# A two-block transformer kernel: own buffers for the first conditioning slabs, and a new order of the work around the first pair of heads

## The chip, the cores and the metric

The kernel runs on one core of a Trainium2 chip. The metric is the device time of one execution in microseconds, as the median of several runs. Beside it there is one profiled execution, whose trace gives the start, the length and the releaser of each instruction.

## The reference

The first block has two layers, the second block one. All tokens: T = 512, width 1024. Layer 0, where the change lies, is a gated delta rule with conditioning:

```python
c_act = jax.nn.silu(c)
mod = c_act @ ada_w[layer] + ada_b[layer]          # 6 parts of 1024
shift_m, scale_m, gate_m, shift_f, scale_f, gate_f = split(mod, 6)
h = rmsnorm(x, norm_mix_g) * (1.0 + scale_m) + shift_m
# gdn_mixer(h): q, k, v, gate, beta and decay are projections of h
#   q, k, v pass a causal convolution of 4 taps and silu; q and k are l2-normed
#   chunked gated delta rule over 8 heads of 128:
#   S_t = exp(g_t)(I - beta_t k_t k_t^T) S_{t-1} + beta_t k_t v_t^T ;  o_t = S_t^T q_t
#   o = rmsnorm(o, norm_g) * silu(gate) ; return o @ w_out
x = x + gate_m * y
h = rmsnorm(x, norm_ffn_g) * (1.0 + scale_f) + shift_f
x = x + gate_f * swiglu(h, w_gate, w_up, w_down)
```

Behind it come a layer of latent attention with its own FFN, and the second block (retention, sliding-window attention, FFN).

## The kernel before, in words

**Slabs.** All weights are cut into slabs of 128 x 2048 fp32 (1 MB). SyncE loads slab s into raw[s % 2] (load_slab, L418), once the low part of slab s - 2 is made. ScalarE copies it to fp32r as its high part (split_hi, L300), once the products of slab s - 2 are done; VectorE subtracts to make the low part (split_lo, L306); TensorE does three matmuls for each 128 x 128 block (lo*H, hi*L, hi*H). A slab is 16 steps of three matmuls in layer 0: eight for its first half (bank half m = 0) and eight for its second (m = 1).

**Conditioning.** There are 48 slabs of ada_w. The first eight (shift_m and scale_m) gate the first norm. TensorE multiplies them by silu(c) held in a padded tile, cpad (first_rows_pe L338, copied by first_act L364, turned into columns by first_cols_pe L356), in four groups g of two slabs. Groups 0 and 2 use the two buffers adar, groups 1 and 3 the tile go, so groups 2 and 3 are loaded only once groups 0 and 1 are through (load_first L371). The other 40 are done on GpSimd: a product by silu(c) and three halving sums per slab (ada_chunks L311, L315 and L317); TensorE then adds over the partitions by four small matmuls (ada_pe L408). Their two buffers are again adar, loaded by load_ada (L424) once TensorE is through with the slab two before. Six such slabs belong to each pair of heads, 24 in all, and 16 to the first FFN. GpSimd begins when gg["tsc"] is signalled (L2056).

**The start.** ScalarE squares the eight chunks of x, TensorE sums them (norm_pe L433), ScalarE takes logarithm and exponential (norm_act L453); norm_first_dve (L384) applies norm, scale and shift group by group and writes hL, ScalarE hH. Squares, norm and padded tile lie in tiles that the pairs use later (fs, kbT, pb, dt).

**The first product and the gates.** Slab 0 yields the raw gates of all eight heads. rows_dve_1 to _4 (L629 to L675) and three activations turn them into cumulative decay and beta, by eight-partition instructions; rows_dve_3 (L648) is ten of them in a chain. rows_pe (L682) transposes them, tsc_dve (L677) stores them, and SyncE spreads them over the partitions through DRAM (rows_out L690, row_in L698) into dt, dtb and qd.

**Pairs of heads.** gdn_pe (L1110), gdn_act (L705) and gdn_dve (L896) hold an order written out by hand. The projections of q, k, v and gate are 16 slabs of 16 steps, 256 steps; the generator product_steps (L1091) yields after each step, and fill(n) (L1114) puts n steps between the other instructions of TensorE. A step at a slab's beginning waits for its low part, and each half for its bank: that is the convolution (conv L900 on VectorE: four taps, from PSUM) of the same half of the slab before it. Slabs 1, 2, 3 are q, k, v of pair 0; 4, 5, 6 those of pair 1; 7 is the query of pair 2. Before pair 0 there are 64 steps (slabs 1 to 4), then 48 in each of pairs 0, 1, 2 and 48 in pair 3.

A pair p (loop at L1138) starts, when the key is scaled (gg["kn"]), with the gram products of the keys (L1153). Six levels then invert a triangular matrix: TensorE multiplies (L1185), ScalarE copies (pb_copy, zz_copy L784 to L790), TensorE multiplies (L1213), VectorE copies under a mask (level L970). Fillers stand on both sides of L1213 (lv_fill). After these come four rounds t over the chunks: value, state product (L1250), output (L1257, L1258), with the state updated by VectorE (state L1000). Meanwhile convolution, activation, sum of squares (sum_squares L1118: square on ScalarE, matmul with ones, Ln into fln, Exp into fex) and scaling (q_norm L929, k_norm L936) prepare pair p + 1. At the end the output norm's two sums (L1274) share one bank, W: the second waits for the logarithm of the first (gg["oln"]).

Of the kernel before, what the change touches and what calls it, by code (L numbers as in the profile page):

```python
# [46 lines left out]
ADA_SKEW = 4  # L47
# [71 lines left out]
def build(nc, slabs, ada, vecs, consts, masks, rope, vbias, pos, xin, out):  # L119
# [4 lines left out]
    with ctx:  # L124
# [29 lines left out]

        gdn = ExitStack()
        lvl = sb("lvl", [P, 7 * P], i32, gdn)
# [19 lines left out]
        go = sb("go", [P, KC, T], scope=gdn)  # L176
        rows, rtmp = go[0:GH, 0:4, :], go[0:GH, 4:7, :]
        cpad = dt[:].rearrange("p m t -> p (m t)")[:, 0:KC * 32].rearrange("p (k n) -> p k n", k=KC)
# [58 lines left out]
        go_in, go_done = [sem("go_in0"), sem("go_in1")], sem("go_done")  # L237
# [96 lines left out]
        def row_summed(eng, g, h):  # L334

            eng.wait_ge(go_done if g % 2 else ada_done, g // 2 * 2 + h + 1)

        def first_rows_pe(pe, g, h):  # L338

            a = Slab(g // 2 * 2 + h)  # L340
            if g % 2:
                pe.wait_ge(go_in[h], a.prior(1, 16))
                w3 = go[:, 4 * h:4 * h + 4, :].rearrange("p c t -> p (c t)")
            else:
                pe.wait_ge(ada_in[h], a.prior(1, 16))
                w3 = adar[h]
# [7 lines left out]
            last.then_inc(go_done if g % 2 else ada_done, 1)  # L354

        def first_cols_pe(pe, g, h):  # L356

            pe.wait_ge(row_ready, 2 * g + h + 1)
            for m in range(2):
                last = T_.matmul(first_bank[g][:, 2 * h + m:2 * h + m + 1], st[:, 2 * h + m, :], ones[:, 0:1],  # L360
                                 start=True, stop=True)
            last.then_inc(first_col, 1)

        def first_act(act, g):  # L364

            for h in range(2):
                row_summed(act, g, h)
                S_.activation(st[:, 2 * h:2 * h + 2, :].rearrange("p a n -> p (a n)"), row_bank[h],
                              ACT.Copy).then_inc(row_ready, 1)

        def load_first(sp, g):  # L371

            for h in range(2):
                src = ada[ADA_FIRST[g][h], :, :]
                if g % 2:
# [329 lines left out]
        def gdn_act(act):  # L705
# [59 lines left out]
            for m in range(2):  # L765
                silu(vs, 3, m)
            split_hi(act, Slab(5))

            for p in range(GH // 2):
# [38 lines left out]

                for m in range(2):
# [66 lines left out]
                w("op", p + 1)  # L876
                for m in range(2):
                    S_.activation(up[:, m, :], D[2][:, m, :], ACT.Square, scale=P ** -0.5).then_inc(gg["osq"], 1)
                    S_.activation(go[:, 2 * p + m, :], D[2][:, m, :], ACT.Copy,
                                  scale=vec[:, V["gdn_g"]:V["gdn_g"] + 1]).then_inc(gg["osq"], 1)  # L880
# [4 lines left out]
                nle()  # L885
                for m in range(2):
                    w("oss", 2 * p + m + 1)
                    S_.activation(vT[:, m, :], D[0][:, 1, :] if not front and m else W, ACT.Ln,
                                  bias=eps).then_inc(gg["oln"], 1)
                for m in range(2):  # L890
                    w("oln", 2 * p + m + 1)
                    S_.activation(vT[:, m, :], vT[:, m, :], ACT.Exp, scale=-0.5).then_inc(gg["oex"], 1)
# [3 lines left out]
        def gdn_dve(dve, chain):  # L896
# [213 lines left out]
        def gdn_pe(pe):  # L1110
# [23 lines left out]
            w("fln", 3)  # L1134
            sum_squares(xi, 1, 4)
            fill(12)

            for p in range(GH // 2):  # L1138
# [4 lines left out]
                lv_fill = 2 if front else 3  # L1143
# [34 lines left out]
                for lv in range(1, 7):  # L1178
# [36 lines left out]
                    if lv in (1, 3, 5):  # L1215
                        ada_at(lv // 2)
# [11 lines left out]
                for t in range(NT):  # L1228
# [1075 lines left out]
```

## Time and profile before

| | |
|---|---|
| median of 3 runs | 2621.35 us (2618.05 to 2631.58) |
| the profiled execution | 2633.81 us, its span 2632.0 us |
| TensorE, matmul | 2433.5 us busy (92%), 11504 instructions |
| VectorE | 1126.2 us (43%) |
| ScalarE | 900.9 us (34%) |
| GpSimd | 354.7 us (13%) |
| DMA | 259.7 MB, mean 99 GB/s |
| chain that ended last | TensorE 73%, issue 10%, GpSimd 7%, VectorE 6%, ScalarE 3% |

Busy time is the sum over an engine's instructions; it doesn't say which of them the end waits for. An "x" with a number is a count of instructions; a releaser in brackets is what ended the idle time before the row. The profile takes a span on the device, and the time of the execution lies 1.8 us above it.

### The profile page before, as it was taken

The page shows a single profiled execution, that of the slowest core. Times are in us where ns is not written, and L with a number is a line of the kernel's source. Part 1 is how long each engine was busy: PE and PEld are TensorE (multiplying, and loading weights), DVE is VectorE, ACT ScalarE, POOL GpSimd, SP SyncE. Part 2 cuts the span into 40 slices and gives each one's busy share as a digit, 9 for nine tenths or more (in the row PEclk, how much of TensorE's full clock was granted, in tenths as well). Part 3 has the DMA queues.
Part 4 walks back from the last instruction along what each step waited for, and adds up shares of the span by engine and source line. Part 5 has one row for each costly group of instructions (what it writes and reads, how often), then busy time and mean ns, then how long its engine had stood idle before and what let it go on. Part 6 is the DMA issues. An engine that isn't in the chain of part 4 may idle for free.

```text
span 2632.0 us, 28942 instructions
## 1 busy us (share of the span) xinstructions
PE 2433.5 (92%) x11504; PEld 1929.2 (73%) x11504; DVE 1126.2 (43%) x1186; ACT 900.9 (34%) x1086; POOL 354.7 (13%) x164
## 2 busy tenths in 40 slices
PE   7899999989999978889999998999987798999997
PEld 4688888768888855567888886877865586788886
DVE  3956754543322464444333235343246524433234
ACT  4455453333311244333332124333234422432122
POOL 0345574357700000000000000000000000000000
PEclk8899999989999988889999998999998799999999
DMA  6324332335422313221222222122210022222222
GB/s 237 135 104 149 124 121 81 108 133 190 161 96 96 112 48 114 94 80 64 96 96 96 96 96 104 62 67 76 96 48 19 32 94 80 80 96 93 99 80 96
DMA packets 38430, 259.72 MB, mean 99 GB/s; under 512 B 4280, under 2 KB 4536, under 8 KB 8144
## 3 DMA queue, kind: packets, MB, share of 16 engines
q1 hardware_dynamic: 38352, 258.59, 27.6%
q8 instruction: 60, 0.98, 0.2%
q14 instruction: 18, 0.15, 0.0%
HBM read 256.42 MB, written 2.15 MB: 98 GB/s over the span
## 4 chain that ended last, share of the span: by engine, by line
PE 73%; issue 10%; POOL 7%; DVE 6%; ACT 3%; DMA 1%; POOLq 0%; DVEq 0%; ACTq 0%; SPq 0%
PE D L260 18%; PE D L261 18%; PE D L262 18%; POOL adar L317 4%; POOL adar L315 3%; PE D L275 3%; PE D L276 3%; PE D L277 3%; PE D L1453 1%; PE D L296 1%; PE D L297 1%; PE D L295 1%; PE D L1452 1%; PE D L1469 1%; DVE lo L308 1%
## 5 line engine op out<-in xcount | busy, mean ns | idle before, releaser
L308 DVE TENSOR_TENSOR lo<-raw,hi 128x2048 fp32r<-128x2048 f32 (+1 forms) x185 | 420.8, 2274 | 463.6 <-ACT hi L304 463.4
L260 PE MATMUL D<-hH,lo 128*128 128x512 f32 x1456 | 585.7, 402 | 0.0
L261 PE MATMUL D<-hL,hi 128*128 128x512 f32 x1456 | 575.4, 395 | 0.0
L262 PE MATMUL D<-hH,hi 128*128 128x512 f32 x1456 | 575.2, 395 | 0.0
L304 ACT ACTIVATE hi<-raw 128x2048 fp32r<-128x2048 f32 (+1 forms) x185 | 342.9, 1853 | 494.3 <-PE D L262 282.9
L260 PEld LDWEIGHTS D<-hH,lo 128*128 128x128 f32 x1456 | 275.1, 189 | 70.4 <-issue 8.0
L261 PEld LDWEIGHTS D<-hL,hi 128*128 128x128 f32 x1456 | 275.2, 189 | 66.6 <-issue 4.0
L262 PEld LDWEIGHTS D<-hH,hi 128*128 128x128 f32 x1456 | 274.7, 189 | 65.0
L317 POOL TENSOR_TENSOR adar<-adar 128x1024 f32<-128x1024 f32 (+2 forms) x120 | 201.8, 1681 | 9.4
L315 POOL TENSOR_TENSOR adar<-adar,cact 128x2048 f32<-128x2048 f32 x40 | 153.0, 3825 | 357.1 <-DMA adar<-in_ada 263.1
L261 PE MATMUL D<-aL,hi 128*128 128x512 f32 x444 | 176.0, 396 | 0.0
L260 PE MATMUL D<-aH,lo 128*128 128x512 f32 x444 | 176.0, 396 | 0.0
L262 PE MATMUL D<-aH,hi 128*128 128x512 f32 x444 | 176.0, 396 | 0.0
L1311 ACT ACTIVATE aH<-af 128x1024 f32 x33 | 35.0, 1060 | 326.3 <-DVE af L1328 326.3
L1328 DVE TENSOR_TENSOR af<-sg,D 128x1024 f32<-128x1024 f32 x33 | 40.3, 1222 | 203.9 <-PE D L262 203.9
L275 PE MATMUL D<-hH,lo 128*128 128x512 f32 x192 | 84.0, 437 | 47.1 <-DVE hL L482 32.6
L1103 PE MATMUL D<-hH,lo 128*128 128x512 f32 x256 | 117.2, 458 | 2.1 <-ACT qs L782 2.1
L506 DVE SCALAR_TENSOR_TENSOR x<-D,mod,x 128x512 f32<-128x512 f32 (+1 forms) x48 | 34.6, 748 | 176.2 <-PE D L262 149.7
L1105 PE MATMUL D<-hH,hi 128*128 128x512 f32 x256 | 102.8, 402 | 0.0
L1104 PE MATMUL D<-hL,hi 128*128 128x512 f32 x256 | 102.7, 401 | 0.0
L1307 ACT ACTIVATE sg<-D 128x1024 f32<-128x1024 f32 x33 | 33.9, 1027 | 200.0 <-PE D L262 160.9
L262 PEld LDWEIGHTS D<-aH,hi 128*128 128x128 f32 x444 | 83.6, 188 | 20.4
(374 smaller groups left out, 3518.2 us busy)
## 6 DMA issues: line engine op xcount, KB each, us to landing
raw<-in_slabs SPq DMA_DIRECT2D x185, 1024.0 KB, 4.8
adar<-in_ada SPq DMA_DIRECT2D x44, 1024.0 KB, 4.8
go<-in_ada SPq DMA_DIRECT2D x4, 1024.0 KB, 11.6
x<-in_xin SPq DMA_DIRECT2D x1, 2048.0 KB, 14.2
dt<-bcast SPq DMA_DIRECT2D x8, 256.0 KB, 3.4
dtb<-bcast SPq DMA_DIRECT2D x8, 256.0 KB, 4.3
qd<-bcast SPq DMA_DIRECT2D x8, 256.0 KB, 7.5
out<-x SPq DMA_DIRECT2D x1, 2048.0 KB, 6.3
```

The costliest lines, as they stand in the source:

```text
L260: T_.matmul(o, lo[s.slot][:, w], H[:, k, :], start=(k == 0), stop=False)
L261: T_.matmul(o, hi[s.slot][:, w], L[:, k, :], start=False, stop=False)
L262: last = T_.matmul(o, hi[s.slot][:, w], H[:, k, :], start=False, stop=(k == kc - 1))
L275: T_.matmul(o, lo[s.slot][:, w], H[:, k, :], start=(k == 0), stop=False)
L276: T_.matmul(o, hi[s.slot][:, w], L[:, k, :], start=False, stop=False)
L304: S_.activation(hi[s.slot][:, 0:n], raw[s.slot][:, 0:n], ACT.Copy).then_inc(hi_ready, 1)
L308: V_.tensor_tensor(lo[s.slot][:, 0:n], raw[s.slot][:, 0:n], hi[s.slot][:, 0:n], ALU.subtract).then_inc(lo_ready, 1)
L315: chain.link(nc.gpsimd.tensor_tensor(r3, r3, cact[:].unsqueeze(2).to_broadcast([P, KC, 2 * P]), ALU.mult))
L317: last = nc.gpsimd.tensor_tensor(r3[:, 0:n], r3[:, 0:n], r3[:, n:2 * n], ALU.add)
L1103: T_.matmul(o, lo[s % 2][:, c], hH[:, k, :], start=(k == 0), stop=False)
L1104: T_.matmul(o, hi[s % 2][:, c], hL[:, k, :], start=False, stop=False)
L1105: last = T_.matmul(o, hi[s % 2][:, c], hH[:, k, :], start=False, stop=(k == KC - 1))
```

## The change

1. The eight first slabs: two in adar, six in a new tile fw, each with its own semaphore, so that none waits for a buffer. Squares, norm rows, norm output, padded tile and copied rows have tiles of their own (xsq, xnt, xrs, cpad, arow), which all lie where the pairs' tiles lie later. SyncE loads x ahead of the slabs; TensorE sums the squares ahead of group 0. adar is used by two slabs fewer before GpSimd's, so ADA_SKEW and ADA0 change.
2. ScalarE makes the high part of slab 2 ahead of the exponential of the gates, VectorE the low part of slab 3 ahead of rows_dve_3.
3. TensorE does 44 + 4 steps ahead of pair 0 and 64 in it (three fillers in place of two, later places for the sums, the conditioning after levels 2, 4 and 6 instead of 1, 3 and 5). The second half of pair 0's value, and the whole query of pair 1, are convolved inside pair 0, and the high and low part of slab 5 are made there.
4. GpSimd waits for gg["kn"] in place of gg["tsc"].

```diff
-ADA_SKEW = 4
+ADA_SKEW = 6
+        fw = sb("fw", [P, 6, SLAB], scope=pre)
+        xsq = sb("xsq", [P, 2, T], scope=pre)
+        xnt = sb("xnt", [P, 2, T], scope=pre)
+        xrs = sb("xrs", [P, T], scope=pre)
+        cpad = sb("cpad", [P, KC, 32], scope=pre)
+        arow = sb("arow", [P, 4, P], scope=pre)
...
         def load_first(sp, g):
             for h in range(2):
                 src = ada[ADA_FIRST[g][h], :, :]
-                if g % 2:
-                    if g > 1:
-                        sp.wait_ge(go_done, h + 1)
-                    sp.dma_start(go[:, 4 * h:4 * h + 4, :].rearrange("p c t -> p (c t)"), src).then_inc(go_in[h], 16)
+                if g:
+                    sp.dma_start(fw[:, 2 * g + h - 2, :], src).then_inc(fw_in[2 * g + h - 2], 16)
                 else:
-                    if g > 1:
-                        sp.wait_ge(ada_done, h + 1)
                     sp.dma_start(adar[h][:], src).then_inc(ada_in[h], 16)
...
             S_.activation(small[0:GH, 0:1], vec[0:GH, V["a_log"]:V["a_log"] + 1], ACT.Exp)
+            split_hi(act, Slab(2))
             act.wait_ge(bank_free[0], 1)
             S_.activation(u_, u_, ACT.Exp, scale=-1.0).then_inc(gg["row"], 1)
             S_.activation(beta, beta, ACT.Sigmoid).then_inc(gg["row"], 1)
-            split_hi(act, Slab(2))
...
             exp_pair(xi, 4)
-            for m in range(2):
-                silu(vs, 3, m)
-            split_hi(act, Slab(5))
+            silu(vs, 3, 0)
...
-                split_hi(act, Slab(6 + 3 * p))
+                split_hi(act, Slab(6 + 3 * p if p else 5))
                 level(1)
+                if p == 0:
+                    silu(vs, 3, 1)
+                    level(2)
+                    silu(q2, Q_SEQ(1), 0)
+                    level(3)
+                    split_hi(act, Slab(6))
+                    silu(q2, Q_SEQ(1), 1)
+                    w("kn", 1)
+                    for m in range(2):
+                        square_unit(q2, fs, m, 7 + m)
+                    level(4)
+                    level(5)
+                    nle()
+                    log_unit(fs, 0, 5)
+                    level(6)
+                    log_unit(fs, 1, 6)
+                    exp_pair(fs, 6)
+                    split_hi(act, Slab(7))
+                    for m in range(2):
+                        zz_copy(6, m)
+                    w("wtp", 1)
+                    S_.activation(pb[:], D[2][:], ACT.Copy).then_inc(gg["wt"], 1)
+                    vn_copy(0)
+                    for m in range(2):
+                        silu(ks, K_SEQ(1), m)
+                    vn_copy(1)
+                    w("qn", 2)
+                    for m in range(2):
+                        square_unit(ks, fs, m, 9 + m)
+                    nle()
+                    vn_copy(2)
+                    log_unit(fs, 0, 7)
+                    decay(1)
+                    split_hi(act, Slab(8))
+                    vn_copy(3)
+                    log_unit(fs, 1, 8)
+                    exp_pair(fs, 8)
+                    out_copy()
+                    for m in range(2):
+                        silu(vs, V_SEQ(1), m)
+                    out_roots()
+                    continue
...
                 conv(qs[0], 0, 0, 1, m)
+            split_lo(dve, Slab(3))
             rows_dve_3(dve, chain)
-            split_lo(dve, Slab(3))
             rows_dve_4(dve)
...
             split_lo(dve, Slab(4))
+            gaps(0)
             conv(vs, 2, 0, 3, 0)
-            gaps(0)
             q_norm(0)
-            conv(vs, 2, 0, 3, 1)
             beta_decay(0)
             k_norm(0)
-            split_lo(dve, Slab(5))
-            conv(qs[1], 0, 1, 4, 0)
...
-                if front:
+                if p == 0:
+                    conv(vs, 2, 0, 3, 1)
+                elif front:
                     conv(qs[x % 2], 0, x, Q_SEQ(x), 1)
                 level(1)
                 k_turned(1)
+                if p == 0:
+                    conv(qs[1], 0, 1, Q_SEQ(1), 0)
+                    split_lo(dve, Slab(5))
...
+                if p == 0:
+                    level(2)
+                    v_turned(0)
+                    level(3)
+                    v_turned(1)
+                    conv(qs[1], 0, 1, Q_SEQ(1), 1)
+                    level(4)
+                    conv(ks, 1, 1, K_SEQ(1), 0)
+                    split_lo(dve, Slab(6))
+                    level(5)
+                    conv(ks, 1, 1, K_SEQ(1), 1)
+                    level(6)
+                    state(0)
+                    split_lo(dve, Slab(7))
+                    conv(vs, 2, 1, V_SEQ(1), 0)
+                    q_norm(1)
+                    state(1)
+                    gaps(1)
+                    state(2)
+                    conv(vs, 2, 1, V_SEQ(1), 1)
+                    beta_decay(1)
+                    split_lo(dve, Slab(8))
+                    k_norm(1)
+                    conv(qs[0], 0, 2, Q_SEQ(2), 0)
+                    continue
...
-            fill(32)
+            fill(44)
             rows_pe(pe)
-            fill(8)
+            fill(4)
             w("tsc", 1)
             sum_squares(fs, 0, 1)
-            fill(4)
             w("fln", 1)
             sum_squares(fs, 1, 2)
-            fill(4)
             w("fln", 2)
             sum_squares(xi, 0, 3)
-            fill(4)
             w("fln", 3)
             sum_squares(xi, 1, 4)
-            fill(12)
...
-                lv_fill = 2 if front else 3
+                lv_fill = 3 if p in (0, 3) else 2
+                late = 1 if p == 0 else 0
...
-                    elif lv == 4 and front:
+                    elif lv == 4 + late and front:
...
-                    elif lv == 5 and front:
+                    elif lv == 5 + late and front:
...
-                    if lv in (1, 3, 5):
-                        ada_at(lv // 2)
+                    if lv in ((1, 3, 5) if p else (2, 4, 6)):
+                        ada_at((lv - 1) // 2)
...
-                    if t == 1 and front:
+                    if t == 1 + late and front:
...
-                    if t == 2 and front:
+                    if t == 2 + late and front:
...
-                    fill(2 if front or t < 2 else 0)
+                    fill(2 + late if front or t < 2 else 0)
...
+            sp.dma_start(x[:], xin[:, :, :]).then_inc(x_in, 16)
             load_first(sp, 0)
-            sp.dma_start(x[:], xin[:, :, :]).then_inc(x_in, 16)
...
             pe.wait_ge(pad_ready, 2)
-            for h in range(2):
-                first_rows_pe(pe, 0, h)
             pe.wait_ge(x_in, 32)
-            for h in range(2):
-                first_cols_pe(pe, 0, h)
-            norm_pe(pe, 0, fs)
-            for g in range(1, 4):
+            norm_pe(pe, 0, xsq)
+            for g in range(4):
...
-            pool.wait_ge(gg["tsc"], 1)
+            pool.wait_ge(gg["kn"], 1)
...
-            first_act(act, 0)
             act.wait_ge(x_in, 32)
             for c in range(KC):
-                square(act, 0, fs, c)
+                square(act, 0, xsq, c)
+            first_act(act, 0)
```

## Rows read from the trace of the kernel before

**Rows 1.** Busy time by stretch: length, then busy (instructions) by engine, PEclk, DMA share, GB/s.
```profile
58.00:124.00 66.00, 54.74 (x219) 42.24 (x218) 55.34 (x59) 30.84 (x33) 20.39 (x8) 0.87 0.33 112
124.00:210.00 86.00, 84.42 (x562) 73.93 (x561) 54.05 (x68) 42.41 (x61) 39.72 (x18) 1.00 0.32 116
```
**Rows 2.** Timeline of the start: start us, us, engine, line, operation, [idle before, releaser].
```profile
36.59 1.93 PE L352 MATMUL D<-go,dt 128*32 128x256 f32 x16 [1.41 <-DMA go<-in_ada]
...
44.38 0.79 PE L275 MATMUL D<-hH,lo 128*128 128x512 f32 x1 [4.05 <-DVE lo L308]
```
**Rows 3.** Busy time by stretch, the start, 27 to 30 us.
```profile
27.00:30.00 3.00, 3.00 (x38) 1.43 (x36) 0.65 (x3) 2.78 (x5) 0.00 (x0) 1.00 0.25 52
```
**Rows 4.** Timelines of VectorE, ScalarE and TensorE, 58 to 112 us; last row: pair 0.
```profile
58.00 0.74 DVE L634 TENSOR_SCALAR go<-D,vec 8x512 f32<-8x512 f32 x1 [7.07 <-PE D L277]
...
71.50 0.74 DVE L906 TENSOR_SCALAR qs<-D,vec 128x512 f32<-128x512 f32 x1
...
74.51 0.67 DVE L655 TENSOR_TENSOR go<-go 8x512 f32<-8x512 f32 x1
...
76.21 1.90 ACT L304 ACTIVATE hi<-raw 128x2048 fp32r<-128x2048 f32 x1
...
84.99 2.27 DVE L308 TENSOR_TENSOR lo<-raw,hi 128x2048 fp32r<-128x2048 f32 x1
...
85.09 0.63 ACT L750 ACTIVATE go<-go 8x512 f32<-8x512 f32 x1 [5.68 <-DVE go L668]
...
87.19 0.67 DVE L674 SCALAR_TENSOR_TENSOR go<-go 8x512 f32<-8x512 f32 x1
...
87.92 1.87 PE L687 MATMUL D<-cst,go 8*128 8x8 f32 x16 [7.65 <-DVE go L674]
...
98.72 0.69 ACT L721 ACTIVATE fs<-D,vec 128x512 f32<-128x512 f32 x1
...
105.60 4.51 DVE L920 TENSOR_TENSOR dt<-dt,cst 128x1024 f32<-128x1024 f32 x1
...
111.83 2.08 PE L1120 MATMUL D<-xi,cst 128*128 128x512 f32 x2 [3.60 <-ACT xi L721]
...
187.66 1.23 DVE L920 TENSOR_TENSOR dt<-dt,cst 128x1024 f32<-128x1024 f32 x1
```
**Rows 5.** Busy time by stretch, behind the two waits; PEclk is the third number from the end.
```profile
88.00:94.00 6.00, 6.00 (x27) 5.12 (x28) 5.79 (x9) 0.71 (x2) 0.00 (x0) 0.54 0.58 161
112.00:118.00 6.00, 6.00 (x14) 4.07 (x15) 5.89 (x7) 4.00 (x5) 3.19 (x3) 0.55 0.00 0
```
**Rows 6.** Timeline of TensorE: the last filler step ahead of the first pair, and its start.
```profile
123.08 0.40 PE L1103 MATMUL D<-hH,lo 128*128 128x512 f32 x1
...
123.78 1.95 PE L1153 MATMUL D<-ks 128*128 128x128 f32 x16
```
**Rows 7.** Timelines of the first pair: SyncE, GpSimd, TensorE, ScalarE.
```profile
143.58 27.88 SPq L427 DMA_DIRECT2D adar<-in_ada  x3
...
150.87 3.61 POOL L315 TENSOR_TENSOR adar<-adar,cact 128x2048 f32<-128x2048 f32 x1 [35.52 <-DMA adar<-in_ada]
154.56 4.56 POOL L317 TENSOR_TENSOR adar<-adar 128x1024 f32<-128x1024 f32 x3
...
153.97 0.50 PE L414 MATMUL D<-cst,adar 128*128 128x1 f32 x4
...
170.60 0.50 PE L414 MATMUL D<-cst,adar 128*128 128x1 f32 x4
...
185.17 0.61 PE L1250 MATMUL D<-vn,kdT 128*128 128x128 f32 x4
...
189.25 0.79 PE L1103 MATMUL D<-hH,lo 128*128 128x512 f32 x1
...
206.76 1.28 ACT L730 ACT_TABLE_LOAD   x1
...
208.88 1.10 PE L1274 MATMUL D<-up,cst 128*128 128x512 f32 x2 [0.33 <-ACT vT L888]
```

More of the change, by code:

```diff
@@ L152, in build @@
         cact = sb("cact", [P, KC], scope=first)
+        pre = ExitStack()
+        fw = sb("fw", [P, 6, SLAB], scope=pre)
[4 more added lines that the diff above has]
+        arow = sb("arow", [P, 4, P], scope=pre)
+        pre.close()
         gdn = ExitStack()
-        lvl = sb("lvl", [P, 7 * P], i32, gdn)
         tsc = sb("tsc", [P, 4, NT, GH], scope=gdn)
@@ L176, in build @@
         go = sb("go", [P, KC, T], scope=gdn)
+        lvl = sb("lvl", [P, 7 * P], i32, gdn)
         rows, rtmp = go[0:GH, 0:4, :], go[0:GH, 4:7, :]
-        cpad = dt[:].rearrange("p m t -> p (m t)")[:, 0:KC * 32].rearrange("p (k n) -> p k n", k=KC)
         bcast = nc.dram_tensor("bcast", (3 * GH, T), fp32, kind="Internal").ap()
@@ L236, in build @@
         row_ready, first_col, pad_ready = sem("row_ready"), sem("first_col"), sem("pad_ready")
-        go_in, go_done = [sem("go_in0"), sem("go_in1")], sem("go_done")
+        fw_in, first_row = [sem(f"fw_in{j}") for j in range(6)], sem("first_row")
         act_chain, dve_chain = sem("act_chain"), sem("dve_chain")
@@ L334, in row_summed @@
         def row_summed(eng, g, h):
-            eng.wait_ge(go_done if g % 2 else ada_done, g // 2 * 2 + h + 1)
+            eng.wait_ge(*((first_row, 2 * g + h - 1) if g else (ada_done, h + 1)))
         def first_rows_pe(pe, g, h):
-            a = Slab(g // 2 * 2 + h)
-            if g % 2:
[L342 to L346, printed above, removed]
+            pe.wait_ge((fw_in[2 * g + h - 2] if g else ada_in[h]), 16)
+            w3 = fw[:, 2 * g + h - 2, :] if g else adar[h]
             if g:
@@ L353, in first_rows_pe @@
                                      start=(r == 0), stop=(r == 1))
-            last.then_inc(go_done if g % 2 else ada_done, 1)
+            last.then_inc(first_row if g else ada_done, 1)
         def first_cols_pe(pe, g, h):
@@ L359, in first_cols_pe @@
             for m in range(2):
-                last = T_.matmul(first_bank[g][:, 2 * h + m:2 * h + m + 1], st[:, 2 * h + m, :], ones[:, 0:1],
+                last = T_.matmul(first_bank[g][:, 2 * h + m:2 * h + m + 1], arow[:, 2 * h + m, :], ones[:, 0:1],
                                  start=True, stop=True)
@@ L367, in first_act @@
                 row_summed(act, g, h)
-                S_.activation(st[:, 2 * h:2 * h + 2, :].rearrange("p a n -> p (a n)"), row_bank[h],
+                S_.activation(arow[:, 2 * h:2 * h + 2, :].rearrange("p a n -> p (a n)"), row_bank[h],
                               ACT.Copy).then_inc(row_ready, 1)
@@ L807, in to_h, with out_copy, out_roots @@
                     S_.activation(hH[:, c, :], go[:, c, :], ACT.Copy).then_inc(hh_ready, 1)
+                def out_copy():
+                    w("op", p + 1)
+                    for m in range(2):
+                        S_.activation(up[:, m, :], D[2][:, m, :], ACT.Square, scale=P ** -0.5).then_inc(gg["osq"], 1)
+                        S_.activation(go[:, 2 * p + m, :], D[2][:, m, :], ACT.Copy,
+                                      scale=vec[:, V["gdn_g"]:V["gdn_g"] + 1]).then_inc(gg["osq"], 1)
+                def out_roots():
+                    nle()
+                    for m in range(2):
+                        w("oss", 2 * p + m + 1)
+                        S_.activation(vT[:, m, :], D[0][:, 1, :] if not front and m else W, ACT.Ln,
+                                      bias=eps).then_inc(gg["oln"], 1)
+                    for m in range(2):
+                        w("oln", 2 * p + m + 1)
+                        S_.activation(vT[:, m, :], vT[:, m, :], ACT.Exp, scale=-0.5).then_inc(gg["oex"], 1)
                 for m in range(2):
@@ L811, in gdn_act @@
                     S_.activation(xi[:, m, :], D[0][:, m, :], ACT.Copy).then_inc(gg["xi"], 1)
-                split_hi(act, Slab(6 + 3 * p))
+                split_hi(act, Slab(6 + 3 * p if p else 5))
                 level(1)
+                if p == 0:
[21 more added lines that the diff above has]
+                    vn_copy(0)
+                    for m in range(2):
+                        silu(ks, K_SEQ(1), m)
+                    vn_copy(1)
+                    w("qn", 2)
+                    for m in range(2):
+                        square_unit(ks, fs, m, 9 + m)
+                    nle()
+                    vn_copy(2)
[6 more added lines that the diff above has]
+                    out_copy()
+                    for m in range(2):
+                        silu(vs, V_SEQ(1), m)
+                    out_roots()
+                    continue
                 if front:
@@ L875, in gdn_act @@
                     to_h(2)
[L876 to L880, printed above, removed]
+                out_copy()
                 if p == 2:
@@ L884, in gdn_act @@
                     to_h(3)
[L885 to L892, printed above, removed]
+                out_roots()
             for c in range(4, KC):
@@ L2074, in _ @@
                     act.wait_ge(xg_ready, c + 1)
-                    S_.activation(hH[:, c, :], pb[:, c % 2, :], ACT.Identity,
+                    S_.activation(hH[:, c, :], xnt[:, c % 2, :], ACT.Identity,
                                   bias=mod[:, c:c + 1]).then_inc(hh_ready, 1)
@@ L2112, in _ @@
             dve.wait_ge(vec_in, 16)
-            V_.memset(cpad, 0.0).then_inc(pad_ready, 1)
+            V_.memset(cpad[:], 0.0).then_inc(pad_ready, 1)
             dve.wait_ge(x_in, 32)
-            norm_first_dve(dve, chain, kbT[:, 0, :], pb)
+            norm_first_dve(dve, chain, xrs[:], xnt)
             split_lo(dve, Slab(1))
```

3 lines of the change are left out of this document (1 added, 2 removed).

## The prediction

> **What bounds the kernel now.** I read the page first (TensorE busy 92% of the span), then busy time by stretch, TensorE's waits, and the timeline of each engine from the start to the end of the first pair. The busy times show where a change can gain. In the 66 us between the first product and the first pair TensorE works 54.7 us; in the first pair it works 84.4 of 86 us [rows 1]. So the first pair is bound by TensorE's own instructions, and the stretch ahead of it by a chain of VectorE and ScalarE work that TensorE waits for twice: 7.65 us for the gate rows, 3.60 us for a logarithm [rows 4]. After each wait the granted clock is about 0.54, its 1.2 GHz level, for some 5.5 us out of six [rows 5], where work takes twice as long: about 2.7 us lost each time. What the edit can win ahead of the pair is therefore at most 7.65 + 3.60 + 5.4 = 16.7 us. At the very start the last pair of conditioning slabs lands at 36.6, and the products begin at 44.4 [rows 2].
>
> All sums are made against the profiled execution (2633.8 us around a span of 2632.0), which lies 12.5 us above the median of 2621.35; I carry the difference over to the median. A difference of 0.5%, 13 us, is what a measurement of this kernel can tell from none.
>
> **Part 1, the eight buffers.** Eight slabs and x are queued without a wait. Before, the third slab buffer was reused, and the DMA engines ran at a quarter of their share around 27 to 30 us [rows 3], since the last two transfers are issued only once the products of the second group are through. x moves ahead, which brings its squares forward, but the last slab remains what comes last, behind the same bytes. The unused share of those 3 us is 2.3 us, and a little lies on either side of them: I take 2.6. From there to the first product (7.8 us of row products, copies, a split on ScalarE, a split on VectorE [rows 2]) nothing changes. **Term: -2.6** (bounds -5 and 0).
>
> **Part 2, the stretch ahead of the first pair.** TensorE now does 48 filler steps here, not 64. A step is 0.70 us [rows 6], so the 16 moved are 11.2 us, and the pair would have to start 11.2 us earlier for this to cost nothing. When can it start? I keep the clock of the profile before. The first product ends at 57.8, the first slab after it (16 steps) at 69.0. The high part of slab 2 moves ahead of the gate's exponential, so VectorE is no longer late: the second half of the query's convolution starts at 69.05, not 71.50, and ends at 72.1 [rows 4]. But the low part of slab 3 now stands ahead of the ten gate operations, and it needs ScalarE's high part, which still follows the query's activation and squares: 76.21 - 2.4 = 73.8, done at 75.7. VectorE, which went straight on before, waits 3.6 us, then splits for 2.3 us [rows 4]: the gate operations start at 78.0 (74.51 before) and end 10.5 later, at 88.5. The two exponentials behind them (0.6 each) lay beside that split and no longer do, so the last gate operation starts at 89.8 in place of 87.19, and all behind it shifts by 2.6 us. TensorE's wait there shrinks from 7.65 to about 2, because 12 fillers lie ahead: that is the design's gain. The key's convolution is bound to VectorE, so the first logarithm starts at 98.72 + 2.6 = 101.3.
>
> Now the four sums of squares stand without fillers between them. Each is a matmul pair, an answer by ScalarE (0.7), and the next. TensorE idles over 4 us ahead of the second, and the one that followed a 3.6 us idle took 2.08 [rows 4]: 102.0 + 3 x 2.8 = 110.4, one exponential of the pair 1.1, the key's scaling 1.2: the pair can start at 112.8. GpSimd's later start is in this: the minimum over 128 x 1024 took 4.51 us beside GpSimd and 1.23 without [rows 4]. That shortens VectorE's side to about 110, which is no longer the later one. So the start moves from 123.78 [rows 6] to 112.8, **-10.9**, against 11.2 of fillers moved into the pair, **+11.2**. The waits ahead of the pair are as long as before, only at other places. Also, the pair now begins at the low clock: **+2.5** (bounds 0 and 3).
>
> Here the Trainium skill (TensorE: Matmul & The Clock Gate, section HAM oscillation) warns that work between repeated idle gaps is run at the low clock again and again, and this trace agrees in its 0.54 [rows 5]; by that rule alone a series of bare sums is a loss.
>
> **Part 3, the first pair.** TensorE was busy 84.4 of 86 us, so fillers cover nothing that was open beyond 1.2 us of small waits: **-1.2**. The new order adds these waits:
> - Query, second half: its convolution follows level 3 on VectorE and its activation and two squares go ahead of level 4's copies on ScalarE. One side is 1.0 + 0.6 + 3.0 + 0.6 + 1.1 + 1.1 = 7.4 to 7.7, TensorE's own is 6.9 (six fillers and the level's products): **+0.8** (0 to 2.5).
> - Conditioning: the low part of slab 6 stood ahead of level 2, now it follows level 4 and a convolution. SyncE queues slab 8's load behind it, and the third conditioning slab behind that. From issue to GpSimd took 7.3 us, and GpSimd 8.2 [rows 7]. Two levels were 16.6 us [rows 7], two more fillers each way make them 19.4; the split ends 6.3 after level 4, leaving 13.1 for 15.9: **+2.8** (0 to 6).
> - Value, first half: step 49 needs its bank, so the convolution behind state 0 and behind the low part of slab 7: 1.1 + 2.3 + 3.0 = 6.5 after the state's product. TensorE got to the corresponding filler in 4.1 [rows 7], now 4.3: **+2.2** (1 to 3).
> - Value, second half: step 57 needs the convolution behind state 2: 3.8 against 2.3 of TensorE's own work, **+1.5** (0 to 4).
> - Output norm: after the output copies ScalarE now loads a table (1.28), does two activations (1.15) and loads the other table before it reads the first norm; before, only the last load stood there [rows 7], and TensorE waited 0.33. **+2.5** (1 to 3.5).
> - GpSimd begins with the pair, beside the identity copy and the masked copy of two SBUF inputs: **+1.0** (0 to 4, the upper end by the 3.3 that contention added to the minimum [rows 4]).
>
> By the Trainium skill (SBUF - State Buffer, Who interferes with whom), a VectorE instruction with two SBUF inputs and a GpSimd one that reads SBUF exclude one another for the whole instruction, and one with PSUM as an input does not. The trace agrees in the 4.51; by it most level copies, which read PSUM, are safe.
>
> Later pairs keep their order: after 112 steps both versions stand at the same filler.
>
> **Sum:** -2.6 - 10.9 + 11.2 + 2.5 - 1.2 + 0.8 + 2.8 + 2.2 + 1.5 + 2.5 + 1.0 = +9.8 us. 2621.35 + 9.8 is about 2631: slightly slower, and within what counts as the same.
>
> **The rivals.** (a) VectorE and ScalarE keep up inside the pair: every wait of part 3 rests on a margin of 1 to 3 us. Without them, -2.6 - 10.9 + 11.2 + 2.5 - 1.2 = -1.0: 2620. For it: VectorE was busy only 54 of 86 us [rows 1]. Against: it works in order, and the waits come from places in the queue. (b) The fillers cover the whole chain ahead of the pair: TensorE waits nowhere there and stays at the high clock: -16.7 - 2.6 = -19.3, 2602, faster. It decides if the key's scaling ends by 96, that is 11.2 + 16.7 us earlier than before. Against it: the gate operations cannot end ahead of 85 and four sums follow them. Something between would do for 13 us. (c) The new waits let the clock fall inside the pair: two of them near 3 us, like the 3.60 after which it was low, with 2.7 us each, and GpSimd's contention at its upper end, +3: 9.8 + 5.4 + 3 = +18, 2639, slower. (d) The edit doesn't do what it says, as when the early transfers are not closer together: 0 for part 1, +12.4.
>
> **How the numbers follow.** Forecast 0.50 (with 0.13 of it beyond +13 us), (a) 0.25, (b) 0.08, (c) 0.14, (d) 0.03, counted as the same. Faster 0.08, same 0.65, slower 0.27. The range runs from a little better than (a), where the two exponentials and the start gain 5 us each, to beyond (c): 2610 to 2645; (b) and the far end of (c) are left out.
>
> **What would show it.** In the changed profile: the last slab's products near 34; the first product near 41.8; VectorE idle ahead of slab 3's low part; TensorE's wait for the gate rows near 2; the first pair's first product near 110, and the second pair's near 219.6, some 109 us later (86.0 before). I am wrong if the first pair takes under 100 us, or if it starts ahead of 105.

## The result and the profile after

| | before | after |
|---|---|---|
| median of 11 runs | 2629.92 us | 2648.43 us |
| profiled execution | 2633.81 us | 2647.41 us |
| ratio, 95% interval | | 1.0077 [1.0065, 1.0089] |

The change makes the kernel 18.5 us slower by the medians. I had forecast +9.8 us. Half of the distance from my 2631 to the measured 2648 is the base: the three runs shown had a median of 2621.35 us, eleven have 2629.92. The other half is the change itself. By the ratio, which is taken over all runs, the change costs 20 us; its interval does not hold 1, so the difference is small but clear of noise.

Busy time by stretch of the kernel after, the stretches that answer to [rows 1]:
```profile
54.50:109.70 55.20, 43.23 (x170) 29.89 (x168) 41.96 (x52) 28.03 (x31) 0.00 (x0) 0.85 0.37 132
109.70:220.10 110.40, 100.47 (x608) 86.46 (x609) 65.65 (x75) 45.74 (x64) 64.17 (x29) 0.96 0.27 101
```
The first number behind the comma is TensorE's busy time. The stretch ahead of the first pair is 11 us shorter and still has 12 us in which TensorE does nothing. The pair holds 110.4 us where it had 86.0, and ten of them are idle.

The start, and what answers to [rows 2], in the timeline after:
```profile
34.20 1.07 PE L355 MATMUL D<-fw,cpad 128*32 128x256 f32 x16 [1.02 <-DMA fw<-in_ada]
...
41.18 0.79 PE L283 MATMUL D<-hH,lo 128*128 128x512 f32 x1 [4.80 <-DVE lo L316]
```
The last slab's products begin at 34.2 (36.6 before), the first product at 41.2 (44.4).

What answers to [rows 4] and [rows 6], from the timelines of VectorE and TensorE after:
```profile
72.49 2.29 DVE L316 TENSOR_TENSOR lo<-raw,hi 128x2048 fp32r<-128x2048 f32 x1 [3.54 <-ACT hi L312]
...
87.20 1.15 PE L686 MATMUL D<-cst,go 8*128 8x8 f32 x16 [1.89 <-DVE go L673]
...
98.72 2.07 PE L1192 MATMUL D<-fs,cst 128*128 128x512 f32 x2 [3.25 <-ACT fs L720]
101.57 2.08 PE L1192 MATMUL D<-xi,cst 128*128 128x512 f32 x2 [0.78 <-ACT fs L720]
104.42 2.08 PE L1192 MATMUL D<-xi,cst 128*128 128x512 f32 x2 [0.78 <-ACT xi L720]
109.69 3.78 PE L1222 MATMUL D<-ks 128*128 128x128 f32 x16 [3.19 <-DVE ks L984]
```
Each step of the forecast is in it: VectorE waits 3.54 us for the high part of slab 3, TensorE waits 1.89 us for the gate rows and not 7.65, the second sum waits 3.25 us for its square, and the last three sums, 2.07 to 2.08 us each at the low clock, follow one another every 2.85 us. The pair starts at 109.7 (110.2 forecast).

TensorE's waits in the first pair after (us in total, times, the longest):
```profile
PE D L1175 <- DVE vs L953: 4.1, 2, 2.3
PE D L1222 <- DVE ks L984: 3.2, 1, 3.2
PE D L1343 <- ACT vT L817: 2.8, 1, 2.8
PE D L413 <- POOL adar L325: 2.2, 1, 2.2
```
L1175 is the filler that waits for the value's convolution, L1343 the second sum of the output norm, L413 the conditioning; L1222 is the pair's own start.

### The profile page after: what moved, and what is told of

Same layout as the page of the kernel before. It is cut to its first block, busy times and chain, and to the rows that moved or that the text cites. A ratio compares the mean times of both kernels' runs of the same rounds, so it can differ in the third digit from the quotient of the medians.

```text
span 2645.6 us, 28941 instructions
## 1 busy us (share of the span) xinstructions
PE 2439.3 (92%) x11504; PEld 1932.9 (73%) x11504; DVE 1123.5 (42%) x1186; ACT 901.2 (34%) x1086; POOL 354.7 (13%) x164
## 4 chain that ended last, share of the span: by engine, by line
PE 72%; issue 9%; POOL 7%; DVE 5%; ACT 3%; DMA 2%; SPq 0%; POOLq 0%; DVEq 0%; ACTq 0%
PE D L268 18%; PE D L269 18%; PE D L270 18%; POOL adar L325 4%; POOL adar L323 3%; PE D L283 3%; PE D L284 3%; PE D L285 3%; DMA fw<-in_ada 1%; PE D L1522 1%; PE D L1521 1%; ACT hi L312 1%; PE D L303 1%; PE D L304 1%; PE D L305 1%
## 5 line engine op out<-in xcount | busy, mean ns | idle before, releaser
L1175 PE MATMUL D<-hH,lo 128*128 128x512 f32 x256 | 114.0, 445 | 6.1 <-DVE vs L953 4.1
```

The source lines that it names most:

```text
L1175: T_.matmul(o, lo[s % 2][:, c], hH[:, k, :], start=(k == 0), stop=False)
```

## The experiments

All timed ratios are to the kernel before, run on the same chip. The table gives, from each run's one profile, where the first pair starts, how long it takes (from its first product to the second pair's), when layer 0's mixer is done (the first product of its output projection), and what is left of the span behind it.

| run | ratio [95%] | first pair at | first pair | mixer done | rest |
|---|---|---|---|---|---|
| before | | 123.8 | 86.0 | 481.8 | 2150.2 |
| c_before | 1.0002 [0.9988, 1.0017] | 123.7 | 86.0 | 477.1 | 2151.8 |
| after | 1.0077 [1.0065, 1.0089] | 109.7 | 110.4 | 491.5 | 2154.2 |
| c_after | 1.0065 [1.0052, 1.0078] | 111.1 | 117.7 | 500.3 | 2146.6 |
| e_buffers | 0.9982 [0.9967, 0.9997] | 121.0 | 86.0 | 475.5 | 2153.1 |
| e_pool | 1.0002 [0.9989, 1.0016] | 118.5 | 94.7 | 482.0 | 2145.0 |
| f_all | 1.0002 [0.9988, 1.0016] | 111.0 | 102.9 | 482.2 | 2148.1 |
| f_fill | 1.0057 [1.0042, 1.0072] | 105.4 | 114.5 | 488.9 | 2151.7 |
| f_value | 1.0053 [1.0033, 1.0073] | 110.4 | 111.4 | 493.2 | 2153.7 |
| f_norm | 1.0065 [1.0042, 1.0089] | 109.9 | 115.3 | 499.9 | 2153.3 |
| f_ada | 1.0073 [1.0053, 1.0092] | 110.2 | 112.0 | 493.2 | 2150.1 |
| f_pool | 1.0081 [1.0065, 1.0097] | 108.5 | 116.6 | 496.5 | 2153.8 |
| best_a | 0.9951 [0.9937, 0.9965] | 106.9 | 100.6 | 468.4 | 2150.0 |
| best_b | 0.9944 [0.9931, 0.9958] | 114.8 | 88.8 | 464.5 | 2144.6 |

**c_before** is the kernel before, unedited.

> The kernel before, run as a variant of itself: it shows how much of a difference is chance. If the granted clock of the later stages is chance, this run's ratio is 1.000 with an interval that holds 1, and its profile's span lies anywhere within 2616 to 2634 us, while the first pair again takes 86.0 us and starts near 123.8. If it is not chance, the third pair takes 93 us again, as in the profile before.

The first two pairs repeat to 0.1 us; the third took 89.1 and not 93.2. So 4 us there are chance. In the last column all kernels have the same code. The two profiles of the changed kernel differ by 7.6 us there, which is chance too; whether all of the 10 us between the rows are is not shown.

The table leaves the later pairs out. The second pair took 86.0 us in both profiles of the kernel before and 88.2 in both of the change. The fourth, up to the mixer's end, took 92.8 and 92.3 us before and 94.7 and 94.8 after.

**e_buffers**: the change's buffers and its order of loads, with the pairs and GpSimd's start as before.

> Only the own buffers of the first eight slabs (with x first) on the kernel before; the order of the pairs and GpSimd's start are as before. Theory A (this part gains what the start shows): first product at 41.2 in place of 44.4, first pair at 120.6, still 86.0 us long, ratio 0.9985 to 0.9990 (3.2 us of 2630). Theory B (this part brings in something that costs later): first pair later than 121, or ratio above 1.000.

The first product comes at 42.3, 1.9 to 2.1 us earlier than in the two profiles before and 1.1 later than I expected (c_after has 42.3 too, after 41.2). The pair starts at 121.0, on the bound between the two theories, 2.7 us earlier than before, and takes 86.0 us. The ratio lies just below theory A's, with an interval of 1 to 9 us. The part is worth 2 to 3 us by the profile and costs nothing.

**e_pool**:
```diff
-            pool.wait_ge(gg["tsc"], 1)
+            pool.wait_ge(gg["kn"], 1)
```


> Only GpSimd's later start (after the key's scaling) on the kernel before. The minimum then takes 1.23 us and not 4.51, and the whole part that GpSimd slowed gets 6 to 7 us shorter on VectorE; TensorE's wait of 3.6 us ahead of the fourth sum should go, and the clock's fall after it (2.7 us): first pair 5 to 6 us earlier, near 118, if 64 fillers still cover the key's scaling (it then ends near 112). Against it: the masked copy at the pair's start meets GpSimd (+1 to +4 in the pair). Ratio 0.998 to 1.000.

The pair starts 5.2 us earlier and takes 8.7 us more: a loss of 3.5 us at the second pair, and no measurable difference in the whole. VectorE, then TensorE, and the busy times around them:
```profile
124.98 6.25 DVE L1022 COPY_PREDICATED zi<-lvl,up 128x512 f32<-128x512 int32 x2
```
```profile
128.53 0.66 PE L1147 MATMUL D<-cst,zi 128*128 128x128 f32 x4 [3.43 <-DVE zi L1022]
131.29 1.12 PE L1147 MATMUL D<-cst,zi 128*128 128x128 f32 x4 [2.10 <-DVE zi L1022]
```
```profile
124.00:140.00 16.00, 10.42 (x53) 8.43 (x52) 12.43 (x11) 5.64 (x9) 8.90 (x5) 0.79 0.24 66
```
Two masked copies whose inputs both lie in SBUF take 6.25 us beside GpSimd and 1.35 without it (best_b). TensorE waits 5.5 us for them, and the granted clock falls to a mean of 0.79. I had left the clock out of my +1 to +4.

**f_all**: the change with four moves.
```diff
                     level(6)
+                    conv(vs, 2, 1, V_SEQ(1), 0)
                     state(0)
                     split_lo(dve, Slab(7))
-                    conv(vs, 2, 1, V_SEQ(1), 0)
...
                     state(1)
+                    conv(vs, 2, 1, V_SEQ(1), 1)
                     gaps(1)
                     state(2)
-                    conv(vs, 2, 1, V_SEQ(1), 1)
...
                     out_copy()
+                    out_roots()
                     for m in range(2):
                         silu(vs, V_SEQ(1), m)
-                    out_roots()
...
+                if p == 0:
+                    load_ada(sp, Slab(a))
                 load_slab(sp, Slab(8 + 3 * p), SEQ.get(8 + 3 * p))
-                for j in range(3):
+                for j in range(0 if p else 1, 3):
```


> The changed kernel with the waits inside the first pair taken away by four moves: the value's two convolutions of the second pair go ahead of state 0 and ahead of the minimum, the output norm's roots go ahead of the value's activations, and in the first pair the third conditioning slab's load goes ahead of slab 8's. Theory A (the waits are the loss): the first pair takes 110.4 - 4.1 - 2.8 - 2.2 = 101.3 us, the second 86 and not 88.2, since the clock no longer falls at its start; ratio to the kernel before 18.5 - 9.1 - 2.1 = +7 us, 1.0028. Theory B (the rest of the loss lies in later stages and has nothing to do with the pairs): the pair is 9 us shorter, the ratio stays at 1.004 or above.

The pair takes 102.9 us, and the whole loss is gone: 1.0002. By the ratios that is 17 to 20 us, more than the 11 us that I expected of the waits and the clock behind the last one, so both theories are off: the waits cost more than their length. c_after shows how. TensorE's idle time in the pair fell from 9.9 to 3.2 us, and 1.9 of that is a wait for GpSimd at the pair's end.

**c_after** is the changed kernel once more.

> The changed kernel once more, as a second sample beside the fast and slow chance of the clock. If its loss is a property of the kernel, the ratio is again 1.006 to 1.009, the first pair again 110.4 us from its first product to the second pair's; from the end of layer 0's mixer to the end of the span the time may be anywhere within 2145 to 2155 us, as in the five profiles so far. If the time behind the mixer is again 2154 us, at the long end, then something of the loss lies there.

The same kernel's first pair took 117.7 us. The waits that differ (the others are those of the profile after, to 0.1 us), then the timelines of VectorE and of TensorE, and the busy times:
```profile
PE D L1175 <- DVE vs L953: 7.4, 2, 3.7
```
```profile
188.20 3.88 DVE L316 TENSOR_TENSOR lo<-raw,hi 128x2048 fp32r<-128x2048 f32 x1
...
199.67 6.75 DVE L963 TENSOR_TENSOR dt<-dt,tsc 128x512 f32<-128x512 f32 x2
```
```profile
195.24 0.76 PE L1175 MATMUL D<-hH,lo 128*128 128x512 f32 x1 [3.72 <-DVE vs L953]
```
```profile
192.00:210.00 18.00, 13.38 (x62) 11.15 (x62) 15.44 (x15) 4.84 (x7) 14.66 (x7) 0.81 0.35 130
210.00:229.00 19.00, 13.86 (x51) 10.00 (x52) 15.50 (x11) 10.30 (x13) 12.19 (x5) 0.80 0.35 136
```
The low part of slab 7 took 3.88 us; in the other profile of this kernel it was 2.43. The rows of c_after's GpSimd, of after's GpSimd, and of after's VectorE:
```profile
186.33 3.60 POOL L323 TENSOR_TENSOR adar<-adar,cact 128x2048 f32<-128x2048 f32 x1
```
```profile
185.05 3.60 POOL L323 TENSOR_TENSOR adar<-adar,cact 128x2048 f32<-128x2048 f32 x1
```
```profile
188.37 2.43 DVE L316 TENSOR_TENSOR lo<-raw,hi 128x2048 fp32r<-128x2048 f32 x1
...
196.71 1.29 DVE L963 TENSOR_TENSOR dt<-dt,tsc 128x512 f32<-128x512 f32 x2
```
The wait for the convolution behind it grew from 2.27 to 3.72 us, as much as the split did, the filler after it ran slow (0.76 us and not 0.48), and the granted clock was 0.81 and 0.80 in the two stretches that follow, where the first profile had 1.00 and 0.99. Ahead of the second wait it was the two subtractions of the gaps, 6.75 us and not 1.29, and that wait was 3.7 us again, not 1.8. Of the 7.3 us between the two pairs 3.3 are idle time of TensorE and 4.0 are busy time, the same work at a lower clock. The time behind the mixer was 2146.6 us, so nothing of the loss is seen there.

GpSimd works beside the split in both, and what differs is the moment. In c_after the split starts 1.7 us before the end of GpSimd's product (188.20 and 189.93), in after 0.3 us before it (188.37 and 188.65). Counted from the pair's start, GpSimd's product begins at 75.4 (after) and 75.2 us (c_after), but the split at 78.7 and 77.1. The split waits for TensorE's chain, and in after the clock had fallen behind TensorE's wait of 2.23 us for GpSimd at 67.2; in c_after, behind 2.12 us, it had not. So in after a short slow stretch made the split late enough to miss most of GpSimd's product.

Six profiles have this order of the pair and both waits: 110.4 (after), 117.7 (c_after), 114.5 (f_fill), 115.3 (f_norm), 116.6 (f_pool) and 112.0 us (f_ada). The profile after is the shortest of them, a lucky case. Four of them have a wait of 3.7 us or more, and the split took 3.88 to 3.94 us; after and f_fill have none, and the split took 2.43 and 2.33. These two are also the only ones in which the clock fell behind the wait for GpSimd (in f_ada there is no such wait).

**f_fill** puts the stretch ahead of the pair back in part.
```diff
-            split_lo(dve, Slab(3))
             rows_dve_3(dve, chain)
+            split_lo(dve, Slab(3))
...
-            fill(44)
+            fill(32)
             rows_pe(pe)
-            fill(4)
+            fill(8)
             w("tsc", 1)
             sum_squares(fs, 0, 1)
+            fill(4)
             w("fln", 1)
             sum_squares(fs, 1, 2)
+            fill(4)
```


> Only the stretch ahead of the first pair is put back in part: the low part of slab 3 again behind the ten gate operations, 32 fillers ahead of the gate rows' transposes, then 8, 4 and 4 between the first sums. Theory A (that order and the bare sums of squares at the low clock ate the gain): the gate operations start about 6 us earlier, the sums take 1 us and not 2 each, and the first pair starts at 102 to 105 in place of 109.7; ratio to the kernel before 5 to 7 us below the change's, about 1.004 to 1.006. Theory B (the key's scaling is bound by VectorE's amount of work): it starts at 108 or later.

The pair starts at 105.4, 4.3 us earlier with the same 48 fillers ahead of it: the order cost that much. Theory B is out. All of the 4.3 us are gained on VectorE, where the low part of slab 3 no longer stands ahead of the ten gate operations: TensorE's transposes of the gate rows start at 82.97 and not at 87.20. From there to the pair's start both kernels take 22.4 to 22.5 us, although the first three sums now take 1.0 us each and not 2.1. So the bare sums at the low clock cost nothing here, and that half of theory A is wrong.

The pair itself is not touched and took 114.5 us. The value's waits, and the busy times of the pair:
```profile
PE D L1175 <- DVE vs L953: 4.0, 2, 2.2
```
```profile
105.40:219.90 114.50, 104.11 (x609) 88.78 (x610) 66.19 (x75) 45.78 (x64) 64.09 (x29) 0.93 0.27 100
```
The waits are as short as in the profile after, 4.0 us against 4.1, and yet the pair is 4.1 us longer, 3.6 of them busy time. The granted clock fell to 0.50, its low level, within 4 us behind each of three waits of 2.30, 2.17 and 1.79 us (GpSimd's sum, the two of the value). In the profile after it fell behind the first of these (2.23) and stayed at 1.00 behind the other two (2.27, 1.80). So a wait need not grow to 3.7 us to bring the clock down: at about 2 us it does so in one execution and not in the next.

**f_value, f_norm, f_ada, f_pool** are the change with one move each: the first two parts of f_all's edit, its third, its last, and `gg["xx"], 2` in place of `gg["kn"], 1` for GpSimd's start.

> The changed kernel; only the value's two convolutions of the second pair move: the first half ahead of state 0, the second ahead of the minimum. Theory A (these two waits, 2.3 us each where VectorE runs free and 3.7 where GpSimd holds its split, let the clock fall in most executions): both waits gone, first pair 105 to 107 us in any execution, and the median falls by more than the 4.1 us of the waits, by 6 to 11 us: ratio 1.003 to 1.005. Theory B (each wait costs its own length): 4 us, ratio 1.0055 to 1.006.

> The changed kernel; only the output norm's roots of the first pair go ahead of the value's activations. The wait of 2.8 us at the pair's end goes, and with it the low clock at the start of the second pair (88.2 to 86.1 us): together 4.9 us, in every execution, ratio 1.0045 to 1.006. If the clock at the second pair's start has another cause, the second pair stays at 88 us and the gain is 2.8 us.

> The changed kernel; only the third conditioning slab's load of the first pair goes ahead of slab 8's. Theory A (SyncE's queue: the load stood behind a wait for slab 6's low part): TensorE's wait of 2.2 us for GpSimd is gone, first pair 108 us. In the kernel with all four moves 1.9 us of that wait were left, so the rival: GpSimd's sum is late for another reason, as the load still stands behind something else, and the wait stays near 2 us; ratio then as the change's, 1.0065 to 1.0077.

> The changed kernel; only GpSimd's start moves, from the key's scaling to the first pair's second masked copy, some 9 us later. The two masked copies take 1.4 us and not 4.3, TensorE's 1.3 us of waits there go. GpSimd's third slab is bound by its load, so the later waits stay. Theory A: first pair 108.5 to 109.5 us in an execution like the first, ratio 1.006 to 1.007. Rival: with GpSimd shifted, its first two slabs are late for levels 2 and 4, and the pair gets longer.

Each took away the wait that it was aimed at, and none brought more than a part of its price in the median.

- f_value: both waits are gone, but TensorE then waited 4.0 us for state 2. VectorE reached it late, behind two subtractions of 4.69 us and a minimum of 3.25 us. The pair took 111.4 us, and the ratio's upper half overlaps the change's.
- f_norm: the wait at the end fell from 2.8 to 0.33 us, but the second pair took 90.4 us, since its two masked copies, 6.33 us beside GpSimd, made TensorE wait 2.1 us; no gain.
- f_ada: the load is issued at 137.7 and not at 161.6, and GpSimd's wait is gone, so the queue was its cause. The rival, that 2 us stay there, fails for this slab; in f_all the 1.9 us stand at the pair's last one. No gain in time, with the other waits in place.
- f_pool: the two masked copies took 1.35 us, and the pair still 116.6. It has the value's long waits (7.4 us), and the profile with such waits is c_after: against its 117.7 the gain is 1.1 us, within what theory A priced (0.9 to 1.9).

The intervals of the last three hold the change's own ratio. By the ratios the four together are worth 17 to 20 us, and each alone between 6 us and nothing, with f_value's 3 to 6 not clear of noise. The costs are not added: in f_value and f_norm a wait that was taken away came back at another place.

**best_a and best_b** take what the runs had shown. Both start GpSimd with `gg["xx"], 2`, behind the masked copies, and move the third pair's `gate(0, 1)` behind its roots. best_a adds this to f_all and f_fill; best_b adds it to e_buffers, with the order of the pairs as before.

> The changed kernel with the four moves that took the waits out of the first pair, with the stretch ahead of it as in f_fill, with GpSimd beginning only after the first pair's two masked copies (so that it meets none of them), and with the second half of the first gate's activation behind the third pair's roots. Theory A: first pair starts near 104 and takes 101 us or a little less; the third pair takes 86 and not 88.5 us, since its 2.8 us wait for a root is gone. Together about 15 us less than the four moves alone minus chance: ratio 0.995 to 0.998.

> The kernel before with three things: the own buffers and x first (-2 to -3 us), GpSimd beginning only after the first pair's masked copies, and the second half of the first gate's activation behind the third pair's roots. If GpSimd's cost in e_pool was the masked copies alone, the first pair starts 5 us earlier, near 115.5, and takes 86 us again, not 94.7; the third pair takes 86 us and not 88.5 to 93. Sum -3 - 5 - 3 = -11 us: ratio 0.994 to 0.997. If GpSimd costs the pair something else, the pair stays over 90 us.

Both beat both kernels: 2618.01 and 2612.85 us, against 2630.92 for the kernel before on the same chip. In each the third pair takes 86.0 us. The fourth takes 88.9 and 88.8 us, some 3.5 less than in c_before, which I had not priced: with the gate behind the roots, its first gate activation needs no table load (1.28 us before), TensorE's wait there is 0.8 us and not 2.1, and the clock is 1.00 at the pair's start, where it was 0.89 to 0.93 over 10 us. In best_a the first pair starts at 106.9, 2.9 us later than I expected. In best_b it starts at 114.8 and takes 88.8, not 86: 2.0 us are idle time (TensorE waits 0.9 us more for the value's scaling, 0.5 for the key's scaled copy and 0.5 for GpSimd), and 0.7 are busy time. best_b is the simpler and at least as fast; their intervals overlap.

## Why the prediction was wrong

**The direction and the stretch ahead of the pair were right.** Forecast 110.2 for the pair's start, measured 109.7 and 111.1; the buffers were priced at 2.6 us and gave 3.2 in the profile after and about 2 in e_buffers and c_after; the 3.6 us behind slab 3's high part were 3.54; 16 fillers moved were paid for by as much idle time, as I had said.

**The waits in the pair had the right places and nearly the right lengths.** Of the profile after, forecast against measured: value 2.2 + 1.5 against 2.3 + 1.8, conditioning 2.8 against 2.2, output norm 2.5 more against 2.5 (0.3 before, 2.8 after), GpSimd's start 1.0 against 0.5. The conditioning's 15.9 is 0.4 above the two rows that it names (7.3 and 8.2), which give 2.4. The query's 0.8 did not come. That the pair took 110.4 us against 109.3 in my sum is in part luck: it is the shortest of six.

**The step that failed is the price of those waits.** I summed each at its own length, with the low clock at the pair's start as the only slow work. TensorE's busy time in the first pair is then 84.4 + 11.2 + 2.5 = 98.1 us. It was 100.5 in the profile after, 104.5 in c_after and 104.1 in f_fill, since the clock fell again behind waits inside the pair. The idle time was near the sum's: 11.2 us by the sum, 9.9, 13.2 and 10.4 measured. I also took GpSimd's contention (+1.0) as a matter of the pair's first instructions. It lies as well on VectorE's split and subtractions beside the state rounds, where it makes 2.3 and 1.8 us of waiting 3.7 each: that and the clock behind them are 7.3 us more in c_after (117.7 against 110.4).

**The later pairs, which I put at nothing, also cost.** The second pair took 2.1 us more in both profiles of the change, behind the output norm's wait of 2.8 us, with a mean clock of 0.61 and 0.64 over its first 4 us (1.00 before). The fourth took 1.9 to 2.6 us more. It has a wait of 2.06 us for ScalarE, in the kernel before as after; behind it the clock stayed at 1.00 in before and c_before and fell to 0.50 in after and c_after. As such a wait goes either way, two profiles each do not show that this is the change's doing.

My rival (c) described just this, two falls of the clock and GpSimd at its upper end, at +18; measured are +18.5. I gave it 0.14. The number also fails by the base: 8.6 us come from a median of three runs. As a difference, +18.5 lies inside what I had allowed (-11 to +24 about the base) and the forecast of +9.8 is still half of it.

Between the two profiles of before and after stand 13.6 us, between the medians 18.5. The profile before had an unlucky third pair (93.2 against 89.1 in c_before), the one after a lucky first. By mixer-done times the change costs 14.4 (after against c_before) to 23.2 us (c_after against c_before), and 18.5 lies between.

**What stays open.** Why the clock falls behind a wait of about 2 us in one execution and not in another was not tried. That such a fall is what decides whether VectorE's split meets GpSimd's product is read from six profiles, and no run moves the one without the other. The rest behind the mixer ranges from 2144.6 to 2154.2 us over fourteen profiles of the same code; why it is long in one execution and short in another was not tried either, and that the change has a part in it is not excluded by these runs. The new order of the pair without the 16 fillers moved into it was not run.

## What to carry to other kernels

Price a wait of the matrix engine by what it may become. One of about 2 us cost its own length in one execution and some 1.8 us more through the clock in another (by the 3.6 us of busy time that two such falls added in f_fill); behind those of 3.5 us or more the clock always fell. And the engine before it in the chain was made late by a third one that nobody waited for. Moving fillers helps only if the chain behind them gets shorter by more than they are worth; first bring forward what the chain waits for, and then move them. And undo such waits together: one by one they showed 0 to 6 us, together 17 to 20.

## What the runs showed of the hardware that I had not expected

In the four pairs of the fourteen profiles the timelines list 29 waits of TensorE between 1.8 and 2.3 us, leaving out one right behind another wait. Behind 14 of them the granted clock went down to its low level, 0.50, within 6 us, and behind the other 15 it stayed at 1.00 (in the profile after 2.23 us went down and 2.27 us did not). Of 18 waits of 2.8 us 14 were followed by the low level, and of 22 waits of 3.5 us or more all were. Behind a fall the clock was low for some 3 to 6 us; the gram products at the first pair's start, 16 matmuls, took 3.78 us at the low level and 1.95 at the high one.

VectorE's two masked copies with both inputs in SBUF took 1.35, 4.34 or 6.25 us depending on where GpSimd's instructions fell, and two subtractions of SBUF tensors 1.29 or 6.75, in two executions of one kernel; three convolution steps, which read PSUM, took 2.31 or 2.32 in both. This agrees with what the Trainium skill (SBUF - State Buffer, Who interferes with whom) says of instructions with two SBUF inputs. The runs add that the same program falls on either side of it from one execution to the next.
